# A two-block network on one core: feed-forward work by tiles of 128 tokens from the first layer on, gate and up loaded side by side

## The reference

```python
# first block, once: x + gated mixer (S5 and gated delta net), x + gated MoE (32 experts, two per token), rms norm
# second block, four layers; D = 1024, D_FF = 2816, S = 256 tokens, fp32
for i in range(4):
    g = norm_g[i]
    x = x + 0.5 * rms_norm(swiglu(rms_norm(x, g[0]), ff1_w_in[i], ff1_w_out[i]), g[1])
    h = rms_norm(x, g[2])
    m = mixer_a(h), mixer_b(h), mixer_c(h)        # i % 3: attention, gMLP, differential attention
    x = x + rms_norm(m, g[3])
    x = x + 0.5 * rms_norm(swiglu(rms_norm(x, g[4]), ff2_w_in[i], ff2_w_out[i]), g[5])

def swiglu(h, w_in, w_out):
    gate, up = split(h @ w_in, 2)                 # 1024 -> 2 x 2816
    return (silu(gate) * up) @ w_out              # 2816 -> 1024
```

## Time and profile before

| | |
|---|---|
| median of 3 runs | 2958.39 us (2953.68 to 2960.48) |
| the profiled execution | 2950.0 us, its span 2948.2 us |
| TensorE busy | 94% of the span, 18450 matmuls |
| VectorE, ScalarE, POOL busy | 54%, 42%, 6% |
| mean granted TensorE clock | 0.972 of full |
| HBM read | 506 MB, 172 GB/s |

### The profile page before, as it was taken

One profiled execution on the slowest core, in us unless ns is written; L12 is line 12 of the kernel. 1 busy time (PEld: TensorE's weight loads), 2 busy tenths in 40 slices (PEclk: granted clock), 3 DMA queues, 4 the chain that ended last, 5 costly groups with the idle time before them and its releaser, 6 DMA issues.

```text
span 2948.2 us, 44334 instructions
## 1 busy us (share of the span) xinstructions
PE 2782.3 (94%) x18450; PEld 2513.5 (85%) x18450; DVE 1600.0 (54%) x1579; ACT 1230.8 (42%) x1436; POOL 177.3 (6%) x278
## 2 busy tenths in 40 slices
PE   7788879999899999999999999999989999999999
PEld 6756877788699987998999998999879989996998
DVE  4893467777554534545455545445445454454544
ACT  2302235656443444434345434334443444345433
POOL 7400000000000000000000000000000000000000
PEclk8898989999999999999999999999999999999999
DMA  7342146878545542655555555554416555543453
GB/s 228 119 138 72 58 160 237 305 276 297 190 164 185 176 146 94 200 186 192 188 169 163 186 185 183 174 185 164 144 59 205 185 179 185 188 154 107 165 185 128
DMA packets 344255, 508.67 MB, mean 173 GB/s; under 512 B 9696, under 2 KB 290304, under 8 KB 344144
## 3 DMA queue, kind: packets, MB, share of 16 engines
q1 hardware_dynamic: 337776, 484.15, 48.9%
q0 software_dynamic: 5792, 20.78, 2.1%
q10 hardware_dynamic: 576, 2.20, 0.2%
HBM read 506.04 MB, written 1.05 MB: 172 GB/s over the span
## 4 chain that ended last, share of the span: by engine, by line
PE 86%; DVE 8%; ACT 3%; DMA 1%; issue 1%; POOL 1%; SPq 0%; DVEq 0%; POOLq 0%; ACTq 0%
PE psum L288 25%; PE psum L289 25%; PE psum L290 25%; PE psum L940 2%; PE psum L2106 1%; DVE act_lo L457 1%; PE psum L2105 1%; DVE raw_r L1627 1%; PE psum L2107 1%; PE psum L2108 1%; DVE arena L1127 1%; PE psum L2138 1%; PE psum L2119 1%; POOL small L371 1%; DVE arena L445 0%
## 5 line engine op out<-in xcount | busy, mean ns | idle before, releaser
L281 DVE TENSOR_TENSOR wlo<-raw,whi 128x2048 fp32r<-128x2048 f32 x331 | 760.5, 2298 | 618.2 <-ACT whi L276 618.2
L288 PE MATMUL psum<-act_hi,whi 128*128 128x256 f32 x3440 | 982.0, 285 | 31.0 <-DVE wlo L281 14.3
L289 PE MATMUL psum<-act_lo,whi 128*128 128x256 f32 x3440 | 979.1, 285 | 0.0
L290 PE MATMUL psum<-act_hi,wlo 128*128 128x256 f32 x3440 | 978.6, 284 | 0.0
L276 ACT ACTIVATE whi<-raw 128x2048 fp32r<-128x2048 f32 x331 | 632.3, 1911 | 393.5 <-PE psum L290 360.2
L288 PEld LDWEIGHTS psum<-act_hi,whi 128*128 128x128 f32 x3440 | 665.9, 194 | 39.5 <-issue 28.5
L289 PEld LDWEIGHTS psum<-act_lo,whi 128*128 128x128 f32 x3440 | 666.2, 194 | 3.0 <-issue 0.2
L290 PEld LDWEIGHTS psum<-act_hi,wlo 128*128 128x128 f32 x3440 | 665.9, 194 | 0.0
L288 PE MATMUL psum<-whi,h_hi 128*128 128x512 f32 x716 | 280.2, 391 | 1.1 <-DVE h_lo L1838 1.1
L290 PE MATMUL psum<-whi,h_lo 128*128 128x512 f32 x716 | 278.6, 389 | 0.0
L289 PE MATMUL psum<-wlo,h_hi 128*128 128x512 f32 x664 | 259.4, 391 | 0.0
(11 more groups left out here) (497 smaller groups left out, 3579.4 us busy)
## 6 DMA issues: line engine op xcount, KB each, us to landing
raw<-in_ff_w_in SPq DMA_DIRECT2D x176, 1024.0 KB, 5.1
raw<-in_ff_w_out SPq DMA_DIRECT2D x88, 1024.0 KB, 4.9
raw<-in_a_w_qkv SPq DMA_DIRECT2D x24, 1024.0 KB, 5.0
raw<-in_w_ada SPq DMA_DIRECT2D x20, 1024.0 KB, 5.2
raw<-in_w_gate SPq DMA_DIRECT2D x35, 512.0 KB, 4.5
raw<-in_w_up SPq DMA_DIRECT2D x35, 512.0 KB, 5.7
raw<-in_w_down SPq DMA_DIRECT2D x28, 512.0 KB, 5.1
raw<-in_c_w_qkv SPq DMA_DIRECT2D x12, 1024.0 KB, 5.2
```

What stands on the lines that cost most here:

```text
L281: dve.tensor_tensor(wlo[s][:], raw[s][:], whi[s][:].bitcast(F32), ALU.subtract).then_inc(lo_ready[s], 1)
L288: pe.matmul(out_ap, lhs[0], rhs[0], start=first, stop=False)
L289: pe.matmul(out_ap, lhs[0], rhs[1], start=False, stop=False)
L290: return pe.matmul(out_ap, lhs[1], rhs[0], start=False, stop=last)
```

## The change

All feed-forward work is done one tile at a time. A pass is (step, tile); there are 22 a feed-forward. The first two steps and the last two are done for tile 0, then for tile 1; in between the tiles alternate. The activations stand still; gate and up of a slab half lie side by side and stream as one run of 512 columns; h comes out with tokens on the partitions and is transposed (`ff_turn`), as in the MoE. The step's first two slabs now hold gate and up of the input dimension's first and second half. Norm, transposes and split of a tile are placed inside the passes of the neighbour block. Mixers do their first four columns tile by tile, the output projection (`wo_pe`) too. All slabs from the MoE on are one stream through eight places (three slots, and areas over the arena), each loaded by two DMAs of half a slab. `keep_clock` remains only behind the MoE. The `Fori` loops of the feed-forward and the mixers are gone. In the gMLP mixer the row sums (`gmlp_sums_pe`) stand behind column 4 (before: behind column 3), `slab_lo` of `wo` 0 stands ahead of the spatial products. The gain rows have a buffer of their own.

```diff
+FF_PASSES = [(0, 0), (1, 0), (0, 1), (1, 1)] + [(i, t) for i in range(2, FF_STEPS - 2) for t in range(2)] \
+    + [(i, t) for t in range(2) for i in (FF_STEPS - 2, FF_STEPS - 1)]
+FF_N = len(FF_PASSES)
+LAST0, LAST1 = FF_N - 3, FF_N - 1
+FFS = [f"ff{l}{h}" for l in range(LAYERS) for h in "ab"]
...
+FF_HEAD = (0, 1, 3, 4)
+FF_SPLIT = {n: [] for n in range(FF_N)}
+FF_SPLIT[1] = [2, 5]
+FF_SPLIT[2], FF_SPLIT[3] = [6], [7]
+for _i in range(2, FF_STEPS - 2):
+    FF_SPLIT[2 * _i] = [3 * _i + 2, 3 * _i + 3]
+    FF_SPLIT[2 * _i + 1] = [3 * _i + 4]
+FF_SPLIT[LAST0 - 1] = [3 * FF_STEPS - 3, 3 * FF_STEPS - 2, 3 * FF_STEPS - 4]
+FF_SPLIT[LAST0] = [3 * FF_STEPS - 1]
...
+RING_A, RING_B = (7, 4, 5, 0, 1, 2, 3, 6), (6, 7, 4, 5, 0, 1, 2, 3)
+PLACE += sorted(range(4), key=lambda p: _used_at[_holder(p)]) + [7, 4, 5, 6]
...
+        def ff_up(pe, f, n, half):
+            i, t = FF_PASSES[n]
+            g = pass_no(f, n)
+            if i == 0:
+                pe.wait_ge(S("act_lo"), act_before(turn_act_index(ff_norm(f))) + 2 * t + half + 1)
+            if half == 0:
+                pe.wait_ge(S("pass_turned_lo"), g - 3)
+            if t == 0:
+                slab_ready(pe, FFS[f], 3 * i + half)
+            hi, lo = (ap.rearrange("p (k n) -> p k n", k=4) for ap in place_of(AT[FFS[f], 3 * i + half])[:2])
+            for c in range(4):
+                k = 4 * half + c
                 ts = slice(t * P, (t + 1) * P)
-                for n in range(2):
-                    ns = slice(n * 512, (n + 1) * 512)
-                    for j in range(2):
-                        ins = three(pe, acc[:, 2 * t + n, :], (hh[:, j, ts], hl[:, j, ts]),
-                                    (hi[:, j, ns], lo[:, j, ns]), first and j == 0, last and j == 1)
-                    if last and not (t and n):
-                        ins.then_inc(S("y_ready"), 1)
-            ins.then_inc(slab_used[GD], 1)
-        def ff_pe(pe, name, n, hb, n_act):
-            b = PLAN.base[name]
-            ff_up(pe, b, hb, 0, act_before(n_act))
-            ff_up(pe, b, hb, 1)
-            ff_down(pe, b, hb, 0, True, False)
-            with pe.Fori(2, n) as i:
-                ff_up(pe, b, hb, i)
-                ff_down(pe, b, hb, i - 1, False, False)
-            ff_down(pe, b, hb, n - 1, False, True)
+                last = three(pe, gate_up(g), (act_hi[:, k, ts], act_lo[:, k, ts]), (hi[:, c, :], lo[:, c, :]), k == 0, k == KD - 1)
+            last.then_inc(S("pass_gu" if half else "half_used"), 1)
+        def ff_turn(pe, f, n):
+            g = pass_no(f, n)
+            pe.wait_ge(S("pass_h"), g + 1)
+            for j in range(2):
+                last = pe.transpose(gate_up(g)[:, j * P:(j + 1) * P], pair_of(h_raw, g)[:, j * P:(j + 1) * P], ident)
+            last.then_inc(S("pass_turned"), 1)
+        def ff_down(pe, f, n):
+            i, t = FF_PASSES[n]
+            g = pass_no(f, n)
+            pe.wait_ge(S("pass_turned_lo"), g + 1)
+            if t == 0:
+                slab_ready(pe, FFS[f], 3 * i + 2)
+            hi, lo = (ap.rearrange("p (j n) -> p j n", j=2) for ap in place_of(AT[FFS[f], 3 * i + 2])[:2])
+            hh, hl = (pair_of(ap, g) for ap in turned_h)
+            for m in range(2):
+                for j in range(2):
+                    js, ms = slice(j * P, (j + 1) * P), slice(m * 512, (m + 1) * 512)
+                    last = three(pe, acc[:, 2 * t + m, :], (hh[:, js], hl[:, js]), (hi[:, j, ms], lo[:, j, ms]),
+                                 i == 0 and j == 0, i == FF_STEPS - 1 and j == 1)
+                if m == 0 and i == FF_STEPS - 1:
+                    last.then_inc(S("y_ready"), 1)
+            last.then_inc(S("pass_down"), 1)
...
+        def ff_pe(pe, f):
+            for n in range(FF_N):
+                ff_up(pe, f, n, 0)
+                if n == 0 and f and f % 2 == 0:
+                    ff_down(pe, f - 1, LAST1)
+                elif n == LAST0 + 1:
+                    ff_down(pe, f, LAST0)
+                elif n not in (0, 2):
+                    ff_turn(pe, f, n - 1)
+                ff_up(pe, f, n, 1)
+                if n == LAST1 and ff_next(f):
+                    turn_pe(pe, ff_norm(f) + 1, 0)
+                if n not in (0, 2, LAST0 + 1):
+                    ff_down(pe, f, n - 1)
+                if n in (1, LAST0, LAST1):
+                    ff_turn(pe, f, n)
+                if n == 1:
+                    turn_pe(pe, ff_norm(f), 1)
+                    ff_down(pe, f, 1)
...
+        def ff_act(act, f):
+            n_in, n_out, nxt = ff_norm(f), ff_norm(f) + 1, ff_next(f)
+            for n in range(FF_N):
+                g = pass_no(f, n)
+                if n == 0:
+                    if f % 2 == 0:
+                        for j in FF_HEAD[2:]:
+                            slab_hi(act, FFS[f], j)
+                        if f:
+                            post_act(act, n_in - 3, 1)
+                    else:
+                        slab_hi(act, FFS[f], FF_HEAD[3])
+                elif n not in (2, LAST0 + 1):
+                    turned_hi_act(act, g - 1)
+                if n == LAST0 + 1:
+                    post_act(act, n_out - 3, 0)
+                if n == LAST1 and nxt:
+                    slab_hi(act, nxt, head_of(nxt)[1])
+                elif n != 1:
+                    for j in FF_SPLIT[n]:
+                        slab_hi(act, FFS[f], j)
+                if n == LAST0 and nxt:
+                    slab_hi(act, nxt, head_of(nxt)[0])
+                silu_act(act, g)
+                if n == 0 and f:
+                    turn_sums_act(act, n_in, 1)
+                if n == LAST0 + 1 and nxt:
+                    turn_sums_act(act, n_out, 0)
+                if n == 1:
+                    slab_hi(act, FFS[f], FF_SPLIT[1][0])
+                    turned_hi_act(act, g)
+                    turn_hi_act(act, n_in, 1)
+                    slab_hi(act, FFS[f], FF_SPLIT[1][1])
+                if n == LAST1 and nxt:
+                    turn_hi_act(act, n_out, 0)
+                if n in (LAST0, LAST1):
+                    turned_hi_act(act, g)
...
+        def mix_heads_pe(pe, l):
+            name, n = f"mix{l}", 3 * l + 3
+            act0 = act_before(turn_act_index(n))
+            for t in range(NT):
+                if t:
+                    turn_pe(pe, n, 1)
+                for j in range(4):
+                    if t == 0:
+                        slab_ready(pe, name, j)
+                    last = proj_n(pe, slab_k(name, j), lambda t: psum[:, 4 + j, t * T:(t + 1) * T], None, None if j else act0, half_of, (t,))
+                    if t:
+                        last.then_inc(S("mix_used"), 1)
+                    elif j == 0:
+                        ff_down(pe, 2 * l, LAST1)
...
+        def wo_act(act, l):
+            n, nxt = 3 * l + 1, f"ff{l}b"
             act.activation(warm, warm, ACT.Silu)
-            if name == "w_out":
-                for j in range(4):
-                    next_hi(act, name, j, 4)
-            else:
-                head_act(act, name, 2)
-                head_act(act, nxt)
-        def wo_dve(dve, name, nxt):
-            if name == "w_out":
-                for j in range(4):
-                    next_lo(dve, name, j, 4)
-            else:
-                head_dve(dve, name, 2)
-                head_dve(dve, nxt, 0)
+            for j in range(2 if KINDS[l] == 1 else 3, 4):
+                slab_hi(act, f"wo{l}", j)
+            post_act(act, n, 0, 0)
+            slab_hi(act, nxt, FF_HEAD[0])
+            post_act(act, n, 0, 1)
+            slab_hi(act, nxt, FF_HEAD[1])
+            turn_sums_act(act, n + 3, 0)
+            post_act(act, n, 1, 0)
+            slab_hi(act, nxt, FF_HEAD[2])
+            turn_hi_act(act, n + 3, 0)
+            post_act(act, n, 1, 1)
...
-                if j in (5, 6):
-                    head_act(act, f"wo{l}", (3, 0)[j - 5])
+                if j in (6, 7):
+                    slab_hi(act, f"wo{l}", j - 6)
...
+            slab_lo(dve, name, 4)
+            dve.wait_ge(S("ws_turned"), 1)
+            dve.tensor_tensor(ws_t, th_view(banks(2)), rep(mat("upto"), GROUPS), ALU.mult).then_inc(S("ws_t"), 1)
+            slab_lo(dve, name, 5)
+            slab_lo(dve, name, 6)
+            dve.wait_ge(S("w_sums"), 1)
+            dve.wait_ge(S("b_rows"), 16)
+            for g in range(GROUPS):
+                gs = slice(g * P, (g + 1) * P)
+                dve.scalar_tensor_tensor(w_sum[:, gs], banks(0)[:, gs], col("ln_b", g), bs_b[:, gs], ALU.mult, ALU.add)\
+                   .then_inc(S("w_part"), 1)
+            dve.wait_ge(S("proj_evac"), proj_base(l) + 4)
+            done(dve.reduce_sum(v_mean, v_part.rearrange("p (t i) -> p t i", t=NT), AX))
+            dve.tensor_scalar(v_mean, v_mean, -1.0 / D, None, ALU.mult).then_inc(S("v_mean"), 1)
+            slab_lo(dve, name, 7)
+            dve.wait_ge(S("v_rstd"), 1)
+            for t in range(NT):
```

(16 more changed lines are left out.)

839 lines of the change are left out of this document (404 added, 435 removed).

## The result

The changed kernel takes **3037.8 us** (median of 4 runs, 3036.0 to 3042.7) where the kernel before, on the same chip, takes 2958.2: a ratio of **1.027** [1.0256, 1.0292], 80 us slower. The forecast was 2957, with 2932 to 2984 for 8 in 10.

What follows compares the result with a forecast made beforehand. TensorE was taken to bound steady steps, a chain of small operations the boundaries. Gains of -88.2 and costs of +86.6 us net -1.6: 2948.4 us profiled, 2957 beside the median; 2932 to 2984 for 8 in 10.

Steps and rivals of the forecast that it cites:

- slab 5: Pass 1 of each feed-forward block: its split, queued behind slab 2's, is needed later and not late; no time added.
- slab 2: Pass 1 of all eight feed-forward blocks: nothing covers its split before the down, TensorE idle 4.77 us each, +38.2 us.
- Clock after the stalls: Matmuls behind gaps of 4.8 us run at 1.2 GHz, 1.5 us lost four times in five: +11 us, bounds 0 and +20.
- Steady passes: 88 steady feed-forward steps, each two passes of 8.44 us: 16.87 us a step against 16.98, -10 us in all.
- rival 2: Passes run as the MoE's do, 0.13 us more each of 176: +24 us, 2981 us; decides from 8.49 us; chance 0.20.
- Rival 3: The 0.8 us slack on even passes is not there, in 56 passes: some +30 us, 2987 us; chance 0.06.
- A wait at a slab's load: Sign against the prediction: it is wrong if TensorE waits at a slab's load; loads were costed at nothing.
- The starts: Seven feed-forward starts: norms run under neighbouring passes, no wait at `turn_pe`, only 1.8 us of transposes stay: -49.5 us.
- the mixers' second tile: Four mixer starts: about 1.1 us between tile 1's transposes and its first matmul; the starts gain 15.8 us in all.
- Block ends: Passes 18 and 19: slabs split ahead of silu make TensorE wait 1.4 and 2.0 us for h, +25.2 us.
- gMLP: gMLP mixer: spatial matmuls wait 5.3 us, output projection starts 8.0 us after the last column where before 2.2; together +11 us.
- MoE to layer 1: From MoE to the first layer: slab places come free some 20 us earlier, the residual starts near 795.1: -7 us.

Runs made afterwards that it cites:

- the dummies: The change with 19 and 20 dummy matmuls ahead of the first two downs of every feed-forward, filling most of both waits: 3008.5 us, 1.0188 of the kernel before.
- the arena's remainder mended: Kernel with slabs 2 and 5 split early (2930.9 us), arena moved to leave 128 by 256; for example, 160 bytes ahead of it: 2908.8 us.
- the layouts: Kernel with slabs 2 and 5 split early (2930.9 us), arena moved in SBUF: directly behind h 2910.4 us, first 2905.8, in the middle 2911.2.

## Why the prediction was wrong

**The step that failed: slab 5.** I wrote that on ScalarE "the turned copy of pass 1, tile 1's turn and slab 5 are queued behind it"; "they are needed later and are not late". No time at which slab 5 is needed stands behind that, and its wait went into the sum with nothing. But pass 1 is already step 1 of tile 0, and `ff_pe` does its down in the same pass, right behind `turn_pe`. The same sentence that priced slab 2 (nothing covers a split that starts behind silu of its own pass) holds for slab 5. It cost 8 x 4.95 = 39.6 us, and taking it away gave 57 us with its clock (2987.4 to 2930.9).

**Clock after the stalls.** The mechanism was right, the size was not: 11 us written, 28.7 in the trace, 25 by the dummies. Behind the eight stalls that I had not seen it is 15.6 us; behind the eight that I had, 13.2, with a loss behind every one and not behind four in five.

**Steady passes.** 8.44 us written, 8.53 measured: 88 x 0.08 = 7 us lost instead of 10 gained. The deciding point of rival 2, 8.49, was passed, but not for its reason. The form of the pass is innocent: with the arena's remainder mended it runs at 8.43, where 8.44 was forecast. Rival 3 did not come either: outside the starts and ends of blocks and the first layer TensorE waits in no pass. What I had read from the earlier trace rows as the price of two runs was the arena under the MoE's stationary blocks, and the new ring puts three of eight places and half of a fourth there. The rule of the Trainium skill that I set against the trace ("TensorE: Matmul & The Clock Gate", the issue gap) gave an estimate of 0.34 us lost a step; 0.08 were lost, and with the arena mended 0.12 are gained, so the rows of before were the better guide here.

**First layer.** A wait at a slab's load, which I had named as a case that would refute me, is there once: 7.2 us and 2.3 of clock. I had looked at the ring in its steady order; in the first feed-forward the places are dealt otherwise, and slab 9 follows slab 5.

**Right.** Slab 2: eight waits, 4.77 us forecast and 4.69 found. The starts: behind the first layer's no wait at `turn_pe`, and no spell at the lower clock is left there; 0.98 us at the mixers' second tile for 1.1. Block ends: 1.4 and 2.0 forecast, about 1.0 and 1.6 found, 20 us for 25. gMLP: 5.3 and 8.0 forecast, 4.81 and 7.68 found. MoE to layer 1: 8.3 us shorter (14.0 for 22.3) where I wrote 7; by the clock time of the start it is 4.8 earlier, since the MoE ended 3.5 later.

**The sum again.** To the forecast 2957 come slab 5 with 39.6, the clock with 28.7 - 11 = 17.7, the passes with 17, the first layer with 9.5, the first feed-forward's start with 2 (4.8 us earlier, not 7), less 5 at the block ends and 1.5 for slab 2 and gMLP: 3036. Measured were 3038, but that this is so close is in part luck. The terms are read from the two profiled executions, and these lie 86 us apart (2950.0 and 3036.0), the medians 80. With the forecast's -1.6 the terms make 78, so 8 us between the profiled executions are not attributed. Whether each of the small terms is right to a microsecond is not shown; the stalls of slabs 2 and 5, their clock and the block ends are, by the runs that take them away, and the passes by the layouts.

## What to carry to other kernels

When work is cut into smaller tiles, follow every loaded operand to its first use in the new order, one by one: an operand whose preparation starts behind the result of the same pass is late by the whole preparation, and "the next step's" may be due at once. Price an idle gap of TensorE with its clock on top: here gaps of 4.7 and 4.95 us cost 28.7 us of clock for 77.1 us of waiting, a third more. And before a layout puts matmul operands into a new buffer, compare the duration of the same matmul on the old and the new one, and the remainders of their addresses.

## What the runs showed of the hardware

A matmul of 512 columns on split fp32 operands takes 0.227 us when the byte addresses of both operands leave 128 by 256, 0.2335 when the arena's operand leaves 224 and 0.2327 when it leaves 0. The 224 costs alike as moving operand (feed-forward) and as stationary one (the MoE: 0.2336, and 0.2278 with the other remainder). Whether the two must leave the same remainder or 128 is good in itself was not tried: no layout moved the other operands' remainder. "SBUF — State Buffer" of the Trainium skill, "Operand start alignment", lets an operand start at any multiple of its element size and says that this is about legality and timed nothing; here all such starts work, and the time differs by 3%.

Moving operands of two runs of 256 columns and of one run of 512 take the same time (1.0290 and 1.0274 of the kernel before, intervals overlapping, passes of 8.53 us in both). A dummy of 128 columns in plain fp32 takes 0.221 us (36 in 7.96) and counts as two instructions in the profile.
